# Chunk rounds of a hybrid block: k times q ahead of the sums of squares of q

## The reference

```
q = q * rsqrt(sum(q*q) + 1e-6) * 128**-0.5          # and k likewise, per head
decay = where(causal, exp(g_i - g_j), 0)
attn_intra = (q @ k.T) * decay
w = solve(I + a_low, k_beta * exp(g)); u = solve(I + a_low, v_beta)
step: v_new = u - w @ S;  o = (q * exp(g)) @ S + attn_intra @ v_new
      S = S * exp(g_last) + k_dec.T @ v_new
```

## Time and profile before

| | |
|---|---|
| median of 3 runs | 1350.14 us (1349.31 to 1351.97) |
| profiled execution | 1349.93 us, span 1348.2 us |
| mean granted TensorE clock | 0.972 |
| PE busy | 1270.4 us (94%) |
| DVE busy | 823.5 us (61%) |
| ACT busy | 455.9 us (34%) |
| POOL busy | 397.2 us (29%) |

### The profile page before, as it was taken

The page is one execution under the profiler, slowest core; times in us unless marked ns, Lnnn a source line. Parts: engine busy times, 40 slices in busy tenths (PEclk is TensorE's granted clock), DMA queues, the critical chain, the costliest instruction groups (busy, mean ns, idle before and its releaser), DMA issues.

```text
span 1348.2 us, 16959 instructions
## 1 busy us (share of the span) xinstructions
PE 1270.4 (94%) x5964; PEld 1005.1 (75%) x5964; DVE 823.5 (61%) x1306; ACT 455.9 (34%) x750; POOL 397.2 (29%) x359
## 2 busy tenths in 40 slices
PE   3899999999799888899999999999999998999998
PEld 3588777887578777754457888888888886888786
DVE  5436777786364656513366665665556568687776
ACT  4231232432222233303244333333333344244342
POOL 3001102340111212100255566565656526200000
PEclk7898999999888999999999999999999998999999
DMA  6411234535721311003222456564468339575634
GB/s 189 127 49 42 75 93 138 153 118 156 234 60 48 98 54 58 0 22 129 80 81 78 162 178 207 188 222 163 147 205 304 108 102 308 181 235 144 201 115 167
DMA packets 188979, 182.60 MB, mean 135 GB/s; under 512 B 19486, under 2 KB 145772, under 8 KB 188908
## 3 DMA queue, kind: packets, MB, share of 16 engines
q1 hardware_dynamic: 188784, 181.64, 42.9%
q10 hardware_dynamic: 124, 0.04, 0.0%
HBM read 123.97 MB, written 56.62 MB: 134 GB/s over the span
## 4 chain that ended last, share of the span: by engine, by line
PE 67%; DVE 17%; issue 6%; ACT 4%; DMA 3%; POOL 2%; SPq 1%; DVEq 0%; ACTq 0%; POOLq 0%
PE ps L2177 29%; PE ps L2182 12%; PE ps L2091 7%; PE ps L1852 6%; PE ps L1967 5%; PE ps L2040 2%; DVE stage L1488 2%; PE ps L2068 2%; PE ps L2056 1%; DVE w_lo L1367 1%; DVE wop_lo L1750 1%; DVE xop_lo L1736 1%; DVE row_stat L1700 1%; DVE stage L1482 1%; POOL mla_sc L901 1%
## 5 line engine op out<-in xcount | busy, mean ns | idle before, releaser
L2177 PE MATMUL ps<-xop_hi,wop_hi 128*128 128x512 f32 x616 | 241.1, 391 | 3.1 <-ACT snap L1308 1.6
L2177 PE MATMUL ps<-xop_hi,wop_lo 128*128 128x512 f32 x616 | 240.1, 390 | 0.0
L2177 PE MATMUL ps<-xop_lo,wop_hi 128*128 128x512 f32 x616 | 240.1, 390 | 0.0
L2177 PEld LDWEIGHTS ps<-xop_hi,wop_hi 128*128 128x128 f32 x616 | 116.0, 188 | 28.8 <-issue 2.6
L2177 PEld LDWEIGHTS ps<-xop_lo,wop_hi 128*128 128x128 f32 x616 | 116.1, 188 | 24.1 <-issue 0.2
L2177 PEld LDWEIGHTS ps<-xop_hi,wop_lo 128*128 128x128 f32 x616 | 115.9, 188 | 24.2
L1750 DVE TENSOR_TENSOR wop_lo<-w_sumS,wop_hi 128x512 fp32r<-128x512 f32 (+1 forms) x104 | 85.7, 826 | 70.6 <-ACT wop_hi L1251 70.6
L2182 PE MATMUL ps<-dop_hi,wop_hi 128*128 128x512 f32 x308 | 121.6, 395 | 6.6 <-DVE x L1814 6.5
L2182 PE MATMUL ps<-dop_lo,wop_hi 128*128 128x512 f32 x308 | 120.8, 392 | 0.0
L2182 PE MATMUL ps<-dop_hi,wop_lo 128*128 128x512 f32 x308 | 120.8, 392 | 0.0
L1852 PE MATMUL ps<-act_hi,w_hi 128*128 128x512 f32 (+1 forms) x352 | 115.8, 407 | 4.3 <-DVE w_lo L1360 3.6
(11 more groups left out here) (280 smaller groups left out, 2140.4 us busy)
## 6 DMA issues: line engine op xcount, KB each, us to landing
w_pair<-in_w_gate_up SPq DMA_DIRECT2D x44, 512.0 KB, 5.4
hidden<-up SPq DMA_DIRECT2D x22, 512.0 KB, 3.0
wd_rows<-in_w_down SPq DMA_DIRECT2D x22, 512.0 KB, 5.3
raw<-in_w_in SPq DMA_DIRECT2D x21, 512.0 KB, 4.5
wd_raw<-down_sums SPq DMA_DIRECT2D x12, 768.0 KB, 8.7
down_sums<-wd_rows SPq DMA_DIRECT2D x33, 256.0 KB, 2.6
wd_raw<-in_w_down SPq DMA_DIRECT2D x9, 768.0 KB, 7.3
qkv_kept<-qkv_st SPq DMA_DIRECT2D x12, 512.0 KB, 5.4
```

The source lines that it names most:

```text
L2177: last = pe.matmul(ps[:, bank, :], w[:, k, :], a[:, k, :], start=(p in ("P1", "P2", "P7") and k == 0 and w is wop_hi[s] and a is hi), stop ...
```

## The change

TensorE's part of the pre stage goes away. Its qk stage now waits for the chunk's load and for the slot's last output, multiplies k by q, and then waits for the squares and does the norms. VectorE's qk stage does the product with the decay first and the small constant second. Before the transposes of the values, TensorE now waits for the small constant's step, since those transposes overwrite the norms' bank. The lists of names follow.

```
-        gp = [Steps(sem(f"gdn_pe{b}"), ["norms", "qk", "kT", "vT", "m0", "x1", "y1", "z1", "x2", "y2",
+        gp = [Steps(sem(f"gdn_pe{b}"), ["qk", "norms", "kT", "vT", "m0", "x1", "y1", "z1", "x2", "y2",
...
-        gd = [Steps(sem(f"gdn_dve{b}"), ["et", "ss", "att", "kd", "vn", "rqs", "r2", "n1", "m1", "n2", "r0", "r", "o1",
+        gd = [Steps(sem(f"gdn_dve{b}"), ["et", "att", "ss", "kd", "vn", "rqs", "r2", "n1", "m1", "n2", "r0", "r", "o1",
...
                     elif stage_name == "qk":
+                        gafter(gp[b], "qk")
+                        dve.wait_ge(e_loaded[b], i * 16 + 16)
+                        gsig(dve.tensor_tensor(attn[b][:, :, :], bank_w, e[:, :, :], ALU.mult))
                         gafter(gp[b], "norms")
                         own("r2", i - 1)
                         gsig(dve.tensor_scalar(sc[:, 0:4], ps[:, U[b], 0:4], EPS, None, ALU.add))
-                        gafter(gp[b], "qk")
-                        dve.wait_ge(e_loaded[b], i * 16 + 16)
-                        gsig(dve.tensor_tensor(attn[b][:, :, :], bank_w, e[:, :, :], ALU.mult))
...
-                    if stage_name == "pre":
+                    if stage_name == "qk":
+                        pe.wait_ge(chunk_loaded[b], i * 16 + 16)
+                        gafter(gd[b], "out", i - 1)
+                        four(W[b], k, q, cnt)
                         gafter(ga[b], "sq")
-                        gafter(gd[b], "out", i - 1)
                         for h in range(4):
                             last = pe.matmul(ps[:, U[b], h:h + 1], kd[b][:, h, :], ones[:, 0:1], start=True, stop=True)
                         last.then_inc(cnt.sem, 1)
-                    elif stage_name == "qk":
-                        four(W[b], k, q, cnt)
                     elif stage_name == "turn":
                         gafter(gd[b], "att")
                         four_t(W[b], k, cnt)
+                        gafter(gd[b], "ss")
                         four_t(U[b], x1, cnt)
```

## The result

The changed kernel takes 1342.36 us (median of 5 runs, 1340.05 to 1344.66) against 1350.55 (1349.31 to 1351.97): 0.9935 of the time before, 95% interval 0.9923 to 0.9946, or 8.8 us less. The forecast was 1345.0 in a range of 1341.0 to 1349.2. The direction, the range and the mechanism held. The gain was larger than forecast (5.1 from the median of 1350.14 that the prediction started from). The profiled execution took 1342.36 us with a span of 1340.6, 7.6 less than the span before.

A forecast was written before the change was run, and what follows sets the result against it. TensorE was taken to bound the kernel, busy 1270.4 of 1348.2 us, so time is won where it stands still or runs slowly. 1349.93 - 5.0 + 2.5 - 2.6 = 1344.8, forecast as 1345.0, range 1341 to 1349.2.

The forecast's parts named there:

- Parts 1 and 2: Second slot: scores of tile 4 start 2.18 us earlier, norms return after k times q at 0.92; -5.0 over four rounds.
- Parts 3 and 4: First slot: first scores wait for qh, gaining 1.2; norms after k times q cost 3.7; +2.5 (-0.4 to +3.7).
- Part 5: VectorE's add and decay product change places; add waits a few tenths of a us, POOL's power starts later; costed at nothing.
- Part 6: Second slot: with the gap before the norms gone, TensorE's clock falls less; -2.6 us, bounds 0 to 3.3.
- The clock gives nothing: Rival: clock falls come as often as before, elsewhere, so only parts 1 to 5 count; 1347.6 us, chance 0.23.
- The pinned chain: Rival, second slot: tile 4's transposes are held by something not passing through the norms; slower, 1356.3 us, chance 0.07.
- Absorbed later: Rival: the rounds' gain meets a load after them that does not move; near 1350 us, chance 0.05.
- The round start gains too: Rival: qh is there when the product before ends, or the round start's clock falls vanish; 1342.1, both 1339.3; chance 0.14.

The follow-up runs named there:

- slot 1 alone: The change made in slot 1 only, slot 0 keeping its norms in the pre stage, against the kernel before: 1338.67 us, ratio 0.9910.
- gap-filled kernel: The kernel before, plus four 128x128 identity products in slot 1's gap ahead of the norms, which still wait for the squares: 1345.83 us, ratio 0.9971.
- Slot 0 alone: The change made in slot 0 only, slot 1 keeping its norms in the pre stage, against the kernel before: 1350.96 us, ratio 1.0008.
- early-squares kernel: The kernel before, with ScalarE squaring q of slot 1 ahead of its copy for slot 0's x2 stage, TensorE's order kept: 1340.56 us, ratio 0.9930.
- the load in halves: The changed kernel with qh loaded in two halves, the upper one half a round earlier: 1338.06 us, 0.9904 of the kernel before.

## Why the prediction was right, and where its sizes were off

**Parts 1 and 2 (slot 1), right and too small.** The term was -5.0. What was mis-sized is "2.18 us earlier" and "their full pace, 0.92". The scores come 485.37 to 487.93 = 2.56 behind the start of the small transposes before, and 483.20 - 482.98 = 0.22 after: 2.34 earlier, since I let them begin only at the end of the row ahead, and rows overlap. The norms behind k times q cost 488.94 - 488.13 = 0.81. With a shorter stretch from scores to transposes (3.55 for 3.63) and 0.05 from the rest, a round gains 1.66 instead of 1.26: 6.6 and not 5.0. The stretches of slot 1 give the same 6.6. By the run times slot 1 alone gained about 12 and the gap-filled kernel 3.9 of clock; the 8 between them is near these 6.6, within the intervals.

**Parts 3 and 4 (slot 0), right in kind; the first round was mis-read.** The term was +2.5. Slot 0 alone measured +1.1 (-0.3 to +2.3), and the change against slot 1 alone about 3, so the two comparisons have the term between them. The traces of before and after can be laid side by side:

- The starts of rounds two to four, from slot 1's keys' transposes of the round ahead to the first scores, took 19.33, 20.10 and 19.85 before, and 19.03, 20.33 and 19.23 after. That is a gain of 0.7, where the prediction had 1.2. qh took over the wait, for 1.06, 1.60 and 0.75.
- From the first scores to slot 0's keys' transposes (before at 409.06, 468.49 and 524.72, after at 409.06, 466.09 and 520.71) these rounds took 10.81, 9.96 and 9.01, and now take 11.46, 10.98 and 9.67: 2.3 more, where the prediction had 3 x 0.92 = 2.8. Together these three rounds cost 1.6, as forecast.
- The first round, where the prediction had one insertion of 0.92 and nothing else, reaches slot 1's small transposes 2.1 later, at 369.83 instead of 367.75. Here the norms run at the low clock:

```profile
347.19 1.71 PE L1990 MATMUL ps<-ones,kd 128*128 128x1 f32 x8
348.76 1.95 PE L2069 MATMUL ps<-V,probsT 128*128 128x64 f32 x8
```

They take 348.76 - 347.19 = 1.57. I had counted 0.92 and named 1.84 as the bound. The mean clock from 336 to 366 us was 0.83 before and 0.72 after. A slow stretch that grows at the start of a round was one of the prediction's signs of being wrong. But the kernels "slot 1 only" and "gap filled", which leave slot 0 alone, also show 0.72 there and reach the small transposes 1.3 later than before. So no run shows that moving slot 0's norms lowers the clock of the first round.

**Part 5, right.** VectorE's add waited for the norms once, 0.8 us. In slot 1 of the third round POOL's power ends at 490.37, and VectorE uses it at 494.23. With VectorE's old order the kernel was no slower.

**Part 6 (the clock), right.** The term was -2.6 of a possible 3.3. The gap filled with work measured 3.9, and the stretches of slot 1 show 3.4 of it. The change got it back whole in slot 1. The advice of the Trainium skill, "TensorE: Matmul & The Clock Gate" (the part on the HAM clock gate), which the prediction set against this term, concerns long idle gaps. Here gaps of 1.26 us, with the norms behind them, were enough in three rounds of four, and filling them kept the clock at 1.00. What the Trainium skill says there of the same kernel's varying from run to run does show. The six runs of the early-squares kernel lie from 1335.46 to 1346.03, with a mean clock of 0.979 in the fastest and 0.970 in the slowest.

**The rivals.** The clock gives nothing: excluded. The pinned chain: excluded, the transposes of tile 4 start 3.77 behind the small ones (486.75 - 482.98), where it had been 6.19 (491.56 - 485.37). Absorbed later: no, the span after the rounds is 1.3 us shorter than before, 775.1 and 776.4 (from the first transposes of the attention's output at 571.76 and 565.51 to the ends at 1348.2 and 1340.6). No run says whether the change did that. The round start gains too: not in the change; it took the load in halves to get that gain. The measured 1342.36 lies near that rival's 1342.1, for another reason: the terms of slot 1 were larger. That the range holds it is partly luck, since its lower part was put there for this rival. In the profiled executions the account closes: slot 1 gains 6.6 + 3.4 = 10.0, the rest of the rounds gives back 1.6 + 2.1 = 3.7, and with the 1.3 behind the rounds that is the 7.6 between the spans. One sum of the prediction is off by 0.1, without a consequence: at 0.9 the pinned chain leaves 7.4 - 3.6 - 1.2 = 2.6 unpaid, not 2.7.

## What to carry to other kernels

When TensorE waits for a small result, ask two questions apart: who is late, and what else could stand in the gap. Here three remedies for the same gap (another place for the norms, earlier squares, dense filler) gave about 12, 9.5 and 3.9 us. The first two take away the wait and the fall of the clock behind it, the third only the fall, so together they show what each cost. Then look for the waits that stay whatever the order (an exponential's chain, a load), and put the moved work there; and before moving work away from the start of a loop, look at what load it had been covering.

## What was unexpected of the hardware

Four dense products a round that compute nothing made the kernel 3.9 us faster, by shrinking an idle gap from 1.26 us to 0.37. And eight passes of one column cost 0.81 to 0.82 us on the path at the full clock and 1.57 in the first round, at the low one. At full clock that is hardly less than the 488.13 - 487.24 = 0.89 of eight passes of 128 columns. Both kinds load weights for every pass (the trace has 64 weight loads for the 64 passes of the norms), which is the likely price; no run here takes the loads away.
